# First layer of the block compression in three fp32r passes over 256 adjacent columns

## What is computed

```python
def compress(rows, params):
    w1, b1, w2, b2 = params
    B, T, G, dh = rows.shape
    n_cmp = (T - CMP_BLOCK) // CMP_STRIDE + 1
    idx = jnp.arange(n_cmp)[:, None] * CMP_STRIDE + jnp.arange(CMP_BLOCK)[None, :]
    blocks = rows[:, idx].transpose(0, 1, 3, 2, 4).reshape(B, n_cmp, G, CMP_BLOCK * dh)
    return jax.nn.gelu(blocks @ w1 + b1) @ w2 + b2
```

## Time and profile before

| | before |
|---|---|
| median of 3 runs | 625.97 us (625.18 to 626.05) |
| profiled execution | 627.12 us |
| its span | 625.4 us |
| TensorE busy | 589.9 us |
| VectorE busy | 310.3 us |
| ScalarE busy | 230.6 us |
| GpSimd busy | 76.5 us |
| TensorE clock granted, mean | 0.991 |

### The profile page before, as it was taken

The page is one execution under the profiler, slowest core; times in us unless marked ns, Lnnn a source line. Parts: engine busy times, 40 slices in busy tenths (PEclk is TensorE's granted clock), DMA queues, the critical chain, the costliest instruction groups (busy, mean ns, idle before and its releaser), DMA issues.

```text
span 625.4 us, 12374 instructions
## 1 busy us (share of the span) xinstructions
PE 589.9 (94%) x5118; PEld 515.0 (82%) x5118; DVE 310.3 (50%) x785; ACT 230.6 (37%) x529; POOL 76.5 (12%) x127
## 2 busy tenths in 40 slices
PE   7899998999899999998999999999999999998993
PEld 5899997887888887997898887666567899997992
DVE  5722224051675223463474656767654447762265
ACT  5543345140323113332332544445353342222333
POOL 0017432020201115404200000000000000000000
PEclk9999998999999999999999999999999999998998
DMA  9347722643612316933722120201111433306104
GB/s 301 140 122 234 263 70 81 254 124 103 204 63 82 105 35 201 309 96 110 262 69 69 48 60 30 68 2 34 35 35 35 124 89 89 114 2 237 35 2 143
DMA packets 45673, 69.99 MB, mean 112 GB/s; under 512 B 4145, under 2 KB 36081, under 8 KB 45362
## 3 DMA queue, kind: packets, MB, share of 16 engines
q1 hardware_dynamic: 38016, 44.84, 23.1%
q0 software_dynamic: 6880, 23.24, 11.2%
q10 hardware_dynamic: 722, 1.12, 0.5%
HBM read 65.22 MB, written 8.13 MB: 117 GB/s over the span
## 4 chain that ended last, share of the span: by engine, by line
PE 88%; DVE 6%; ACT 3%; DMA 2%; issue 1%; ACTq 0%; SPq 0%; DVEq 0%
PE m L1530 53%; PE s L1697 10%; PE s L1821 4%; PE o L1835 4%; PE t L1828 3%; PE t L1672 2%; PE t L1723 2%; DMA U<-in_x_p 2%; PE m L1611 2%; DVE U L1274 1%; PE s L1737 1%; PE o L1782 1%; PE t L1661 1%; ACT U L903 1%; PE o L1808 1%
## 5 line engine op out<-in xcount | busy, mean ns | idle before, releaser
L1530 PE MATMUL m<-h_hi,w_hi 128*128 128x272 f32 x448 | 133.1, 297 | 0.0
L1530 PE MATMUL m<-h_hi,w_lo 128*128 128x272 f32 x448 | 129.2, 288 | 0.0
L1530 PE MATMUL m<-h_lo,w_hi 128*128 128x272 f32 x448 | 128.7, 287 | 0.0
L1530 PE MATMUL m<-w_hi,h_hi 128*128 128x256 f32 (+2 forms) x360 | 104.9, 291 | 3.6 <-DVE U L1478 2.0
L1530 PE MATMUL m<-w_lo,h_hi 128*128 128x256 f32 (+2 forms) x360 | 102.5, 285 | 0.0
L1530 PE MATMUL m<-w_hi,h_lo 128*128 128x256 f32 (+2 forms) x360 | 102.4, 284 | 0.0
L1530 PEld LDWEIGHTS m<-h_hi,w_hi 128*128 128x128 f32 x448 | 84.2, 188 | 10.0 <-issue 7.3
L1164 DVE TENSOR_TENSOR w_lo<-raw,w_hi 128x1024 fp32r<-128x1024 f32 (+2 forms) x62 | 71.2, 1156 | 37.4 <-ACT w_hi L916 37.3
L1530 PEld LDWEIGHTS m<-h_hi,w_lo 128*128 128x128 f32 x448 | 84.5, 189 | 0.0
L1530 PEld LDWEIGHTS m<-h_lo,w_hi 128*128 128x128 f32 x448 | 84.5, 189 | 0.0
L1530 PEld LDWEIGHTS m<-w_hi,h_hi 128*128 128x128 f32 (+1 forms) x360 | 68.4, 190 | 5.5 <-DVE U L1478 2.3
(11 more groups left out here) (278 smaller groups left out, 885.8 us busy)
## 6 DMA issues: line engine op xcount, KB each, us to landing
raw<-in_w_in SPq DMA_DIRECT2D x36, 512.0 KB, 4.0
U<-in_x_p SPq DMA_DIRECT2D x8, 512.0 KB, 7.1
raw<-in_w_o SPq DMA_DIRECT2D x8, 512.0 KB, 4.1
raw<-in_w_in SPq DMA_DIRECT2D x8, 256.0 KB, 3.8
U<-in_ck_win POOLq DMA_DIRECT2D x8, 256.0 KB, 3.4
U<-in_cv_win POOLq DMA_DIRECT2D x8, 256.0 KB, 5.9
raw<-in_w_pa SPq DMA_DIRECT2D x8, 256.0 KB, 4.1
raw<-in_w_pb SPq DMA_DIRECT2D x4, 512.0 KB, 3.4
```

Of the source, the lines that this page charges most:

```text
L1530: ins = mm(out, lhs(a, k), rhs(b, k), start=(k == 0 and a + b == 0), stop=(k == n - 1 and a == 1))
```

## The change

1. **First layer.** A chunk is now two batches (4 tiles) or the prompt: NCH = 10, chunk 0 the prompt's keys, 1 to 4 keys, 5 the prompt's values, 6 to 9 values. Cached rows are loaded with their even groups of 8 rows ahead of the odd (`CMP_ROW`), so that a slice of the first layer reads 256 adjacent columns, from column 0 or from column 1: 2 heads x 2 batches x 64, of which 63 count. ScalarE rounds a tile to `xt_hi`, VectorE subtracts to `xt_lo` and only then frees the bank. Of the fourth tile VectorE makes half of `xt_hi`. `w1` is split likewise (`w1hi`, `w1lo`), keys' behind the prompt's layer, since `w1_lo` lies over `w1`, values' behind the last key pass. `("hidh", c)` multiplies xt_hi with w1_hi and w1_lo, 32 products; `("hidl", c)` xt_lo with w1_hi, 16 products, and stands behind the first two tiles of the next chunk. The prompt's layer stays in fp32 (`hid`).
2. **Main groups.** One for each pair of batches, halved: `("half", ...)` does the first four slices ahead of the third tile, `("main", ...)` the rest behind it.
3. **All tiles are freed by VectorE** (`t_uses`).
4. **Order.** Slots ZA0, ZA1 stand ahead of U0, U1. ln2 and sp are spread over chunks 6 to 9. At the start the square of the sample rows comes ahead of hT of tile 1; C0's weights are split one group earlier. The prompt is first in the ring (`LOADS`), in two DMAs, issued behind the first rope.
5. Addresses in the arena move by 8 columns, the page table comes twice, `WARM` (0 before) goes.

```diff
...
+         ("ZA0", "tr", C_ZA, 256), ("ZA1", "tr", C_ZA, 256),
          ("U0", "tr", C_U, 256), ("U1", "tr", C_U + 256, 256),
-         ("ZA0", "tr", C_ZA, 256), ("ZA1", "tr", C_ZA, 256),
...
+CMP_ROW = 2 * (np.arange(P) % 64) + np.arange(P) // 64
...
-BETWEEN_ROWS = {0: (0, 1, 0, 1), 1: (0, 1, 0, 1), 3: (0, 1, 0, 1), 4: (0, 1, 1, 1)}
-BEFORE_LAST_HIDDEN, AFTER_LAST_HIDDEN = 1, 1
+NCH = 10
+PAIRS = [c for c in range(NCH) if c % 5]
+IN_PROMPT_CHUNK, AFTER_LAST_HIDDEN = 1, 1
...
-    order += [("hT", 1), ("low", 1, 0), ("split", 1, 1), ("low", 1, 1), ("sq", NT), ("sq", 2), ("sq", 3), ("ms", 2, NT)]
+    order += [("sq", NT), ("hT", 1), ("low", 1, 0), ("split", 1, 1), ("sq", 2), ("low", 1, 1), ("sq", 3), ("ms", 2, NT)]
...
-    main(4)
+    main(3)
     order += [("split", 2, 0)]
     main(1)
-    order += [("low", 2, 0), ("split", 2, 1)]
-    main(1)
-    order += [("low", 2, 1)]
+    order += [("low", 2, 0), ("split", 2, 1), ("low", 2, 1)]
+    main(2)
     order += [("out_cmp",), ("wsT",), ("rope", 0)]
     main(4)
     order += [("load_w1",)]
...
-    for c in range(6):
-        for n in range(8 if c % 3 < 2 else 1):
-            order += [("xt", c, n)]
-            if n % 2:
-                if c == 4 and n == 3:
-                    order += [("sp", i) for i in range(NT + 1)]
-                main(BETWEEN_ROWS[c][n // 2])
-            if c and n == (1 if c % 3 < 2 else 0):
-                order += [("kc", c - 1)]
-        if c == 3:
-            order += [("ln2", i) for i in range(NT + 1)]
-        if c == 5:
-            main(BEFORE_LAST_HIDDEN)
-        order += [("hid", c)]
+    order += [("w1hi", 0)]
+    for c in range(NCH):
+        behind = [("hidl", c - 1)] if c - 1 in PAIRS else []
+        if c % 5 == 0:
+            order += [("xt", c, 0)] + behind
+            main(IN_PROMPT_CHUNK)
+            if c:
+                order += [("w1hi", 1), ("w1lo", 1), ("kc", c - 1)]
+            order += [("hid", c)]
+            if c == 0:
+                order += [("w1lo", 0)]
+            continue
+        order += [("xt", c, 0), ("xt", c, 1)] + behind + [("half",) + groups[state["n"]][1:], ("xt", c, 2)]
+        main(1)
+        n = order.index(groups[state["n"] - 1]) + 1
+        after = order[n:]
+        del order[n:]
+        order += [("xt", c, 3), ("kc", c - 1), ("hidh", c)] + after
+        order += {6: [("ln2", i) for i in range(3)], 7: [("ln2", i) for i in range(3, NT + 1)],
+                  8: [("sp", i) for i in range(3)], 9: [("sp", i) for i in range(3, NT + 1)]}.get(c, [])
+    order += [("hidl", NCH - 1)]
     main(AFTER_LAST_HIDDEN)
-    order += [("kc", 5)]
+    order += [("kc", NCH - 1)]
...
+LOADS = [(w, b) for w in ("kc", "vc") for b in ["p"] + list(range(NB))]
...
-                if (w, b) == ("kc", "p"):
-                    pool.wait_ge(cmp_out, 32)
                 slot, done = ring[:, n % RING, :], ring_loaded[n % RING]
                 if b == "p":
-                    src = pk_cmp if w == "kc" else pv_cmp
-                    pool.dma_start(ring[0:64, n % RING, :], src.rearrange("(m r) c -> m (r c)", r=8)).then_inc(done, 16)
+                    pool.wait_ge(cmp_out, 32)
+                    src = (pk_cmp if w == "kc" else pv_cmp).rearrange("(m o r) c -> o m (r c)", o=2, r=8)
+                    for o in range(2):
+                        pool.dma_start(slot[32 * o:32 * o + 32, :], src[o, :, :]).then_inc(done, 16)
                 else:
                     src = {"kc": ck_cmp, "vc": cv_cmp}[w]
-                    pool.indirect_dma_start(slot, None, src, bass.IndirectOffsetOnAxis(rows_sb[:, b:b + 1], 0)).then_inc(done, 16)
+                    pool.indirect_dma_start(slot, None, src, bass.IndirectOffsetOnAxis(cmp_rows[:, b:b + 1], 0)).then_inc(done, 16)
...
+                elif kind == "w1hi":
+                    act.wait_ge(w1_loaded[s[1]], 16)
+                    if s[1]:
+                        act.wait_ge(hid_sum, 5)
+                    else:
+                        act.wait_ge(t_done, T_AT[("qTs",)] + 1)
                         act.wait_ge(out_done, 16 * (N_OUT - 1))
                         act.wait_ge(cmp_out, 32)
-                    for dst, src in xt_parts(c, n, TB[t % 2]):
-                        ins = nc.scalar.copy(dst, src)
-                    ins.then_inc(t_act, 1)
-                elif kind == "hid":
+                    for k in range(2):
+                        ins = nc.scalar.copy(w1_hi[k][:, :, :], w1_at[s[1]][:, 8 * k:8 * k + 8, :])
+                    ins.then_inc(w1_hi_done, 1)
+                elif kind == "xt" and s[1] in PAIRS:
+                    c, n = s[1], s[2]
+                    b, r = divmod(n, 2)
+                    act.wait_ge(t_done, t + 1)
+                    if c > 1:
+                        act.wait_ge(hid_half, PAIRS.index(c))
+                    for g in range(G - n // 3):
+                        ins = nc.scalar.copy(turned(xt_hi, r, g, b), TB[t % 2][64 * g:64 * g + 64, :].rearrange("p (q o n) -> p q o n", q=4, o=2))
+                    ins.then_inc(xt_hi_done, 1)
+                elif kind in ("hid", "hidl"):
                     c = s[1]
-                    b1 = pm("b1k" if c < 3 else "b1v")
-                    if c:
-                        act.wait_ge(kc_done, c)
+                    s_in, s_out = S[c % 2][:, 0:2 * NCP], hid_at[c % 2][:, 0:2 * NCP]
+                    if kind == "hidl":
+                        s_in, s_out = S[c % 2][:, 0:256], hid_at[c % 2]
+                    b1 = pm("b1k" if c < 5 else "b1v")
+                    if c >= 2:
+                        act.wait_ge(kc_done, c - 1)
                     else:
                         act.wait_ge(rope_step, ROPE_STEPS[3])
-                    if c % 3 < 2:
-                        for g in range(G):
-                            act.wait_ge(hid_sum, hid_count(c) + g + 1)
-                            nc.scalar.activation(hid[:, g, :], S[g][:, 0:252], ACT.Gelu_apprx_tanh, bias=b1).then_inc(hid_ready, 1)
-                    else:
-                        act.wait_ge(hid_sum, hid_count(c) + 1)
-                        nc.scalar.activation(hid[:, 0, 0:2 * NCP], S[0][:, 0:2 * NCP], ACT.Gelu_apprx_tanh, bias=b1).then_inc(hid_ready, 1)
+                    act.wait_ge(hid_sum, c + 1)
...
+                elif kind == "w1lo":
+                    dve.wait_ge(w1_hi_done, s[1] + 1)
+                    dve.wait_ge(hid_sum, 5 if s[1] else 1)
+                    if s[1] == 0:
                         dve.wait_ge(out_done, 16 * (N_OUT - 1))
                         dve.wait_ge(cmp_out, 32)
-                    for dst, src in xt_parts(c, n, TB[t % 2]):
-                        ins = v.tensor_copy(dst, src)
+                        v.tensor_copy(xt_sb[:, :].rearrange("p (x n) -> p x n", x=2)[:, :, 2048:2050], ident[:, 0:4].rearrange("p (x n) -> p x n", x=2))
+                    for k in range(2):
+                        ins = v.tensor_tensor(w1_lo[:, 8 * k:8 * k + 8, :], w1_at[s[1]][:, 8 * k:8 * k + 8, :], w1_hi[k][:, :, :].bitcast(F32), ALU.subtract)
+                    ins.then_inc(w1_lo_done, 1)
+                elif kind == "xt":
+                    c, n = s[1], s[2]
+                    b, r = divmod(n, 2)
+                    tb = TB[t % 2]
+                    dve.wait_ge(t_done, t + 1)
+                    if c % 5 == 0:
+                        for r in range(2):
+                            for g in range(G):
+                                ins = v.tensor_copy(xtp[64 * r:64 * r + 64, :, g, :],
+                                                    tb[64 * g:64 * g + 64, 256 * r:256 * r + 256].rearrange("p (q m) -> p q m", q=4))
+                        ins.then_inc(t_dve, 1)
+                        continue
+                    if c > 1:
+                        dve.wait_ge(hid_sum, c - (c == 6))
+                    if n == 3:
+                        if c > 1:
+                            dve.wait_ge(hid_half, PAIRS.index(c))
+                        v.tensor_copy(turned(xt_hi, r, 1, b), tb[64:128, :].rearrange("p (q o n) -> p q o n", q=4, o=2)).then_inc(xt_hi_dve, 1)
+                    dve.wait_ge(xt_hi_done, 4 * PAIRS.index(c) + n + 1)
+                    for g in range(G):
+                        if n == 3 and g == 1:
+                            dve.wait_ge(xt_hi_dve, PAIRS.index(c) + 1)
+                        ins = v.tensor_tensor(turned(xt_lo, r, g, b), tb[64 * g:64 * g + 64, :].rearrange("p (q o n) -> p q o n", q=4, o=2),
+                                              turned(xt_hi, r, g, b).bitcast(F32), ALU.subtract)
                     ins.then_inc(t_dve, 1)
...
+                    ks = range(KD // 2) if kind == "half" else range(KD // 2, KD) if s in HALVED else range(KD)
...
+                elif kind in ("hidh", "hidl"):
+                    c = s[1]
+                    out = S[c % 2]
+                    first = kind == "hidh"
+                    if first:
+                        pe.wait_ge(w1_hi_done, c // 5 + 1)
```

(18 more changed lines are left out.)

234 lines of the change are left out of this document (113 added, 121 removed).

## The result

The changed kernel takes **636.04 us** (median of four runs, 632.97 to 640.52) against 626.01: a ratio of 1.0169, 95% interval 1.0104 to 1.0234. It is slower: the whole interval lies above 1, and in microseconds it reaches from 6.5 to 14.6. The forecast was 618.6, with a range of 612.5 to 625.5, and gave "slower" a chance of 0.10. The profiled execution took 634.68 us with a span of 632.9, where the forecast's sum gives a span of 618.05: 14.85 are to be explained.

The account below looks back on a forecast made before the run. It took TensorE, busy 589.9 of 625.4 us, as the bound; -8.8 (rewritten stretch), -0.45 (earlier weight split) and +1.9 (table loads) sum to -7.35, taken off 625.97: 618.6, range 612.5 to 625.5.

Parts of the forecast that it names:

- The product: First layer: three single-instruction products at 0.118 us each replace two fp32 instructions at 0.227; 12.7 us less TensorE work.
- The table loads: Four more on ScalarE, two in the first sample group's chain: +1.9 us, at best 0, at worst 2.6.
- The start of the kernel: Ahead of the rewritten stretch, C0's weight split moves earlier and a main group's wait goes: -0.45 us.
- Rivals 3, 4 and 5: Odd-column products at 0.227 (639, chance 0.06); weight loads pacing products (624.7, 0.06); chain's table loads costing twice (621.2, 0.05).
- rival 1: Fourth tile's copy and table loads hidden, idle in the rewritten stretch about 7 us: 612 to 614, chance 0.12.
- The granted clock there is 0.99: Rewritten stretch, query transposes to first key tile (132.3 us): clock read as 0.99, with no term for a lower one.
- The term of the pairs: Pairs of batches in the compression: 11.7 us per key pair, 12.2 per value pair, TensorE waiting 0.6 and 1.0.
- Rival 2: Evacuation chain sets each pair: VectorE operations take 0.84, a pair grows 1.2, eight pairs 9.6: 628 us, chance 0.1.
- The ZA product: Value pairs: VectorE's 0.44 us product comes in between, the group is 0.2 longer, TensorE's wait 1.0.
- The start: From query transposes to first hi passes: prompt tile, hidden layer, weight split and first pair in a row; idle 3.6 us.
- The change of weights: Between key and value pairs, with first value pair: 23.0 us, TensorE waiting 3.0, and 1.0 at the hi passes.
- Behind the sample products: From first sample products to the end of the span: 346.4 us, as in the profile before.

Follow-up runs that it names:

- passes_only: Kernel before with each first-layer product replaced by three 256-column fp32r products, compressed values not computed, all around them unchanged: 615.43 us, ratio 0.9805.
- keep_busy: Changed kernel with idle products on TensorE at places where it stood still, nothing left out: 629.39 us, ratio 1.0049 to the kernel before.
- busy_all: keep_busy with idle products also ahead of the first sample products and of the second by-rows group of w_o: 629.00 us, ratio 1.0034.
- before_busy2: Kernel before with idle products behind the query transposes and eight ahead of the second by-rows group of w_o: 625.69 us, ratio 0.9987.
- prompt_first: Changed kernel with the prompt's tile turned ahead of the query transposes: 633.31 us, ratio 1.0095 to the kernel before.
- act_all: Changed kernel with ScalarE making both halves of the fourth tile of xt_hi, VectorE none: 627.57 us, ratio 1.0028 to the kernel before.
- before_busy: Kernel before with idle products behind the query transposes and nine ahead of the first by-rows group of w_o: 629.85 us, ratio 1.0052.

## Why the prediction was wrong, step by step

**What held.** The product: 0.117 us on an even column and 0.120 on an odd one, for 0.118, so 12.7 us of TensorE work went; passes_only confirms some 10.7 of run time. The table loads: 48.44 us from the first key tile to the sample products against a forecast of 48.6. The start of the kernel: 0.9 earlier at the end of the query transposes instead of 0.45, and 0.5 in keep_busy. Rivals 3, 4 and 5 fell, and rival 1 with the result.

**The step that had no term: the clock was taken as given.** The forecast reads "The granted clock there is 0.99" and prices every piece of the changed stretch at full speed, while the same text adds idle time: 3.6 at the start, 3.0 at the change of weights, about 2 ahead of the sample products. At each of these three places the trace of after has a stretch at 1.2 GHz right behind. The window of before at 102 to 106 (0.57) already had the pattern, inside the mean of 0.99. keep_busy takes back 6.6 us without making any wait of the real work shorter, and the difference between busy_all and before_busy2 leaves 3.3 of 10.0. No rival named it. What the runs don't show is a price for each wait: equal waits of 1.2 and 1.3 us were followed by half the clock in after and by the full clock in prompt_first, keep_busy and act_all, so such a term could only have been a range.

**The term of the pairs was mis-sized.** Forecast 11.7 and 12.2, measured 12.73 and, with the clock at 1.00 (keep_busy), 13.18: 3.1 us for the key pairs and about 3 for the value pairs. The chain was the one described (lo pass, subtractions, third tile, copy, subtraction, half copy, hi passes), but each link was priced from a row in the middle of a run. The rows that would have told are the ones at a hand-over, where an engine starts on what another has just finished. One of them, from the chain of before:

```profile
134.31 0.66 PE t L1672 x4
```

A tile behind a wait takes 0.66 for 0.435. The 0.25 of a first product shows in the chain of after. Rival 2 had the right place, the evacuation chain sets each pair, and its +1.2 a pair is near the +1.0 measured, but by luck: its reason, operations at 0.84, did not come. Subtractions took 0.689 on average, and the hand-overs made up the difference. The ZA product was rightly placed ahead of the half copy, and act_all shows that this copy should not have been on VectorE at all: 4.3 us ahead of the sample products.

**The start.** Forecast 14.4 from the transposes to the first hi passes; 18.3 measured, of which 2.7 is the clock (keep_busy) and 1.2 hand-overs. **The change of weights**: 24.3 for 23.0, sums, root, copies and subtractions in the order forecast, each link a little longer. **Behind the sample products** +2.2, of which 1.5 is gone in keep_busy, where the clock stayed at 1.00.

**The sum.** In the profiled execution: about 5.5 clock (span 632.9 against keep_busy's 627.5), some 6 pairs, 1.3 change of weights, 1.2 start, the rest of 14.85 under 1. The median of after lies 1.4 above its profiled execution, and before's 1.1 below, which adds 2.5 to the miss; runs with lower mean clock are the longer ones (640.52 has 0.972, 632.97 has 0.983).

**What stays open.** Why some executions have a stretch at 1.2 GHz at 18 to 22 us and others not, and why one wait of 1.34 us was followed by one and an equal wait not, was not tried. How much of the remaining 4.4 us to passes_only a second `xt_lo` would give was not tried either: there is no room for it.

## What to carry to other kernels

When an edit puts a wait in front of TensorE, price it as a range: from the wait alone to the wait with the lower clock behind it. The same kernel's trace tells what that costs, if the granted clock is read in windows of a few us and not as a mean over the stretch. Run the kernel often enough to see both cases. A chain over three engines is priced from rows at its hand-overs, not from rows in the middle of a run, and a copy in it belongs to the engine that is free at that moment. Moving a step out of such a chain helps only if nothing else that waits there takes its place, which the queue behind it tells.

## What the runs showed that was not expected

- Idle products make the kernel faster: keep_busy executes more than after and takes 629.39 for 636.04. At a place where TensorE does not stand nine of them cost (before_busy: its span grew by 1.2 us behind the first key tile).
- A stretch at 1.2 GHz costs nothing where a load ends later anyway: the tile at 108.12 in before is at 108.16 with the clock at 1.00.
- In after, waits of 1.22 and 1.34 us, with TensorE partly busy around them, went with low clocks of some 10 and 3.5 us (102 to 112, 286 to 290). In prompt_first (1.23, until 100.91), keep_busy and act_all (1.34 each) such waits were followed by a clock of 1.00, and in passes_only a wait of 0.86 until 149.69 was followed by 1.2 GHz from 152 on. The length of the one wait before it does not tell whether the clock falls.
